# Delta-rule outputs for two chunks at once: state products first, masked-score products behind them, as two tiles side by side

## What is computed

```python
def step(S, inp):
    qd, kc, val, att, kt, cd = inp
    v_new = val - jnp.einsum('bhcd,bhde->bhce', kc, S)
    o = jnp.einsum('bhcd,bhde->bhce', qd, S) + jnp.einsum('bhij,bhje->bhie', att, v_new)
    S = S * cd[..., None, None] + jnp.einsum('bhcd,bhce->bhde', kt, v_new)
    return S, o
...
_, o = lax.scan(step, S0, xs)
```

## Time and profile before

| | |
|---|---|
| median of 3 runs | 1151.25 us (1151.17 to 1151.34) |
| the profiled execution | 1147.58 us, of which its span is 1145.8 us |
| busy in the span | PE 1117.3 us (98%), PEld 850.9 (74%), DVE 601.9 (53%), ACT 515.0 (45%), POOL 194.8 (17%) |
| the granted clock of TensorE over the span | 0.994 |
| the stretch of the delta rule's loop | about 146 to 172 us |

### The profile page before, as it was taken

One profiled execution on the slowest core, in us unless ns is written; L12 is line 12 of the kernel. 1 busy time (PEld: TensorE's weight loads), 2 busy tenths in 40 slices (PEclk: granted clock), 3 DMA queues, 4 the chain that ended last, 5 costly groups with the idle time before them and its releaser, 6 DMA issues.

```text
span 1145.8 us, 18715 instructions
## 1 busy us (share of the span) xinstructions
PE 1117.3 (98%) x7673; PEld 850.9 (74%) x7673; DVE 601.9 (53%) x885; ACT 515.0 (45%) x851; POOL 194.8 (17%) x132
## 2 busy tenths in 40 slices
PE   8999999999899999999999999999999999999996
PEld 7987778999688888878888885666666666666663
DVE  5988666879865695695656642222222222222223
ACT  6666553755364665745556342222222222222223
POOL 1339950422554140400000000000000000000000
PEclk9999999999899999999999999999999999999998
DMA  9862724567648656564448579999999999999994
GB/s 312 271 219 81 289 82 170 198 232 283 220 149 291 221 178 232 162 228 156 147 148 325 191 280 421 421 423 423 425 422 420 424 424 422 426 422 423 426 422 182
DMA packets 82700, 332.04 MB, mean 290 GB/s; under 512 B 4555, under 2 KB 6926, under 8 KB 66110
## 3 DMA queue, kind: packets, MB, share of 16 engines
q1 hardware_dynamic: 81236, 328.43, 74.1%
q0 software_dynamic: 1088, 2.34, 1.1%
q10 hardware_dynamic: 298, 0.11, 0.0%
HBM read 329.83 MB, written 1.05 MB: 289 GB/s over the span
## 4 chain that ended last, share of the span: by engine, by line
PE 77%; DVE 8%; DMA 7%; POOL 3%; issue 2%; ACT 2%; SPq 1%; DVEq 0%; ACTq 0%; POOLq 0%
PE bank L1113 18%; PE bank L446 11%; PE bank L448 10%; PE bank L447 10%; PE bank L1132 9%; PE bank L1103 5%; DMA ring<-in_w_exp_down 3%; POOL ring L2671 3%; DMA ring<-in_w_ada 2%; DVE ring_r L1847 2%; DMA ring<-in_w_in 2%; DVE arena L1927 2%; PE bank L1160 1%; PE bank L573 1%; PE bank L1161 1%
## 5 line engine op out<-in xcount | busy, mean ns | idle before, releaser
L1847 DVE TENSOR_TENSOR ring_r<-ring,arena_r 128x2048 fp32r<-128x2048 f32 x93 | 226.2, 2442 | 127.4 <-ACT arena_r L1333 125.7
L1333 ACT ACTIVATE arena_r<-ring 128x2048 fp32r<-128x2048 f32 x93 | 177.3, 1916 | 149.0 <-PE bank L448 69.7
L2671 POOL TENSOR_TENSOR ring<-ring 128x512 f32<-128x512 f32 x84 | 146.2, 1765 | 219.6 <-ACT ring L1424 191.6
L448 PE MATMUL bank<-arena_r,actT_r 128*128 128x512 f32 x384 | 150.5, 392 | 0.0
L446 PE MATMUL bank<-arena_r,tok_r 128*128 128x512 f32 x352 | 140.7, 400 | 1.7 <-DVE con L2312 1.7
L447 PE MATMUL bank<-ring_r,tok_r 128*128 128x512 f32 x352 | 138.2, 393 | 0.0
L2484 DVE TENSOR_TENSOR arena<-bank,arena 64x512 f32<-64x512 f32 x62 | 42.7, 688 | 175.3 <-PE bank L1132 174.6
L446 PE MATMUL bank<-tok_r,arena_r 128*128 128x256 f32 x352 | 99.5, 283 | 1.8 <-DVE actT_r L1864 1.2
L448 PE MATMUL bank<-tok_r,ring_r 128*128 128x256 f32 x352 | 98.3, 279 | 0.0
L447 PE MATMUL bank<-actT_r,arena_r 128*128 128x256 f32 x352 | 98.2, 279 | 0.0
L1304 ACT ACTIVATE arena<-bank 128x512 f32<-128x512 f32 (+5 forms) x123 | 54.4, 469 | 86.5 <-PE bank L1120 50.3
(11 more groups left out here) (426 smaller groups left out, 1833.1 us busy)
## 6 DMA issues: line engine op xcount, KB each, us to landing
ring<-in_w_in SPq DMA_DIRECT2D x22, 2048.0 KB, 9.2
ring<-in_w_exp_down SPq DMA_DIRECT2D x22, 2048.0 KB, 21.4
ring<-in_w_exp_gate SPq DMA_DIRECT2D x21, 2048.0 KB, 22.0
arena<-in_w_exp_up SPq DMA_DIRECT2D x21, 2048.0 KB, 23.6
ring<-in_w_ff SPq DMA_DIRECT2D x16, 2048.0 KB, 7.9
ring<-in_w_ada SPq DMA_DIRECT2D x12, 2048.0 KB, 10.9
arena<-in_w_exp_gate SPq DMA_DIRECT2D x11, 2048.0 KB, 21.6
arena<-in_w_exp_down SPq DMA_DIRECT2D x10, 2048.0 KB, 21.3
```

Source lines behind the costliest of these rows:

```text
L448: return mm(o, l[1], r[0], start=False, stop=stop)
L1333: A(hi, w, ACT.Copy).then_inc(S["w_high"], 1)
L1847: TT(half(i, ringR)[0], w, hi.bitcast(fp32), ALU.subtract).then_inc(S["w_rest"], 1)
L2671: i = nc.gpsimd.tensor_tensor(w[:, k, :], w[:, k, :], w[:, k + n, :], ALU.add)
```

## The change

`do0` to `do3` become two jobs, `do0` and `do1`, one for each half. A job is issued behind `sn1` (for the first half) and behind `vp3` and its fillers (for the second). It first runs all state products of the half, head by head, the two chunks alternating, and then all masked-score products, the two chunks alternating. The two chunks write to partitions 0 to 63 and 64 to 127 of one bank. Since chunk 2's state product now comes after the attention values and the first transposes of the finished tokens, the second state buffer moves to a place that those don't overwrite. ScalarE copies 128 partitions by 512 twice instead of 64 partitions by 512 four times. VectorE waits for one copy instead of two.

```diff
-        states = [KBE[:, 0:512], AT[:, 0:512]]
+        states = [KBE[:, 0:512], qT[:, 512:1024]]
...
+            def chunk_outputs(t):
+                bk = begin(f"do{t}")
+                chunks = [(2 * t + x, C * x) for x in range(2) if 2 * t + x]
+                for h in range(DH):
+                    for n, r in chunks:
+                        mm(bk[r:r + C, h * P:(h + 1) * P], block_cols(qdT)(4 * t + h, r),
+                           states[(n - 1) % 2][:, h * P:(h + 1) * P], start=(h == 0), stop=False, skip_group_check=True)
+                for h in range(DH):
+                    for r in (0, C):
+                        i = mm(bk[r:r + C, h * P:(h + 1) * P], within(MT)(4 * t + h, r), block_rows(VN)(4 * t + h, r),
+                               start=(h == 0 and t == 0 and r == 0), stop=(h == DH - 1), skip_group_check=True)
+                end(i, f"do{t}")
...
-                bk = begin(f"do{n}")
-                for h in range(DH):
-                    o = (4 * t + h) * P
-                    if n:
-                        mm(bk[r:r + C, h * P:(h + 1) * P], qdT[:, o + r:o + r + C], old[:, h * P:(h + 1) * P],
-                           start=True, stop=False)
-                    i = mm(bk[r:r + C, h * P:(h + 1) * P], MT[r:r + C, (4 * t + h) * C:(4 * t + h + 1) * C],
-                           VN[r:r + C, o:o + P],
-                           start=(n == 0), stop=True)
-                end(i, f"do{n}")
-                if n == 0:
-                    prob_turn(range(4))
+                if n % 2:
+                    chunk_outputs(t)
+                else:
+                    prob_turn(range(4)) if n == 0 else None
...
-            def o_copy(n):
-                t, r = n // 2, C * (n % 2)
-                bk = wait_full(act, f"do{n}")
-                done(copy(odn[r:r + C, t * 512:(t + 1) * 512], bk[r:r + C, :]), f"do{n}")
+            def o_copy(t):
+                bk = wait_full(act, f"do{t}")
+                done(copy(odn[:, t * 512:(t + 1) * 512], bk[:, :]), f"do{t}")
...
-            o_copy(0)
             prob_copies((0, 2))
             prob_copies((4, 6))
-            o_copy(1)
+            o_copy(0)
...
             w_high(F0 + 2)
-            o_copy(2)
             w_high(F0 + 3)
             o_high(0)
-            o_copy(3)
+            o_copy(1)
             o_scale(1)
...
                     if n == 2:
-                        wait_full(dve, "do1")
+                        wait_full(dve, "do0")
...
             def o_squares(t):
-                for n in (2 * t, 2 * t + 1):
-                    wait_read(dve, f"do{n}")
+                wait_read(dve, f"do{t}")
```

## The result

The changed kernel is slower: over 20 executions of each, the ratio to the kernel before is 1.0024, 95% interval 1.0014 to 1.0034 (medians 1152.06 against 1148.74 us). Run again beside ten more, it was 1.0019 (1.0005 to 1.0033). The forecast was 2.1 us faster; the two ratios stand for 2.8 and 2.2 us slower, and their intervals reach from 0.6 to 3.9 us.

A forecast was written before the change was run, and what follows sets the result against it. TensorE, busy in all 26.0 us around the loop, was taken as the bound: 5.6 us less work, less waits of 1.7 + 0.2 + 1.6 = 3.5, gives 2.1; 1151.25 - 2.1 = 1149.15 us, range 1147.4 to 1150.9.

The forecast's parts named there:

- Price of the products: Output jobs: state and masked-score groups overlap at 1.02 us each, 2.04 per job, taking 5.6 us of work off TensorE.
- The rival without overlap: Output jobs: masked-score products don't run side by side, 0.85 us more per half, total 1150.0 or 1150.2; chance 0.10.
- the price for every change of tile: Output jobs: alternating tiles costs like a size change, `do1` 5.76 us, 1.9 us slower, 1153.2; chance 0.06.
- Shift of the first half: Up to new state 2: 3.90 us removed ahead of `sn2`, 2.04 added, so `sn2` starts 1.86 us earlier, at 157.46.
- the wait of 1.7: Behind `sn2`, TensorE idles 1.7 us until VectorE has formed state 2; `vp3` starts at 160.26.
- VectorE as the next bound: Second half: VectorE's list ends at 170.03, TensorE idles 1.6 us, first product with `w_out` starts at 170.13.
- The clock: Rival: TensorE falls to 1.2 GHz after the last wait, gain only 0.1 us (1151.1); chance 0.09 shared with later stages.
- the later stages: Rival: transfers ending the program shift by 1 us or more, at worst 2 us slower; chance 0.09 shared with clock.
- All of the gain through to the end: Behind the first product with `w_out`: lists are the same, loads move with TensorE, so all 2.08 us reaches the end.

The follow-up runs named there:

- the wait filled: Changed kernel plus eight idle products, result unread, ahead of the fourth chunk's wait for the state (`vp3`); ratio to the kernel before 0.9994 (0.9980 to 1.0007).
- the kernel with half the idle products: Changed kernel plus four idle products instead of eight ahead of the fourth chunk's wait, leaving 0.56 us of wait; ratio to the kernel before 0.9987 (0.9969 to 1.0006).
- the two-group version: Changed kernel with the third chunk's output products moved behind `sn2`, the fourth's left behind the transposes, in one bank; ratio to the kernel before 0.9986 (0.9975 to 0.9998).
- 16 idle products of 128 by 128 by 128: Changed kernel plus sixteen idle products behind the 1.65 us wait and ahead of `vp3`; ratio to the kernel before 1.0040 (1.0021 to 1.0058).
- the outputs in the old, alternating form: Kernel before, four separate output jobs kept, third chunk's output moved behind the first token transposes so the wait opens; ratio to the kernel before 1.0081 (1.0059 to 1.0103).
- Denser work just ahead: Changed kernel plus eight idle products ahead of `sn2`, the 1.65 us wait left as it was; ratio to the kernel before 1.0028 (1.0013 to 1.0042).

## Why the prediction was wrong, step by step

- **Price of the products: right.** 1.02 us each for 16 side-by-side records, at full clock, and 2.04 for the first job, as taken from the earlier trace rows. Both side-by-side groups at full clock stand in the trace with the wait filled (165.93, 166.95, 167.97). The rival without overlap is refuted: masked-score products of two row tiles into one bank take 1.02 (153.46 to 154.48), not 1.87. So is the price for every change of tile, 5.76 for such a group. Where the Trainium skill ("TensorEngine Tiling (Array Packing)", "Restrictions and Gotchas") says that row tiles can't access the same bank at the same time, the measurement decides, for tiles on the diagonal.
- **Shift of the first half, 1.86 us, and the wait of 1.7: right.** `sn2` at 157.46 and `vp3` at 160.27 against 157.46 and 160.26; the wait is 1.65.
- **VectorE as the next bound: right as a mechanism, where the clock stays up.** With the wait filled the product starts at 169.88, forecast 170.13, after 1.25 us of waiting, forecast 1.6. In the changed kernel itself it is hidden behind a slower TensorE.
- **The clock: this step failed.** The prediction had it among the rivals, with 0.09 shared with the later stages, and set it aside because in 113 to 117 us TensorE waited 1.6 us and kept 2.4 GHz. That one row was no evidence for a wait at another place: the clock keeps its level over some waits of about this length and falls over this one. It also looked for the fall behind the last wait only, and took its price, 1.95, from 3.9 us of work at half clock behind another wait. It came at the first wait, with `vp3`, the attention values and the outputs behind it, and lasted 13.7 us in one trace and 10.2 in the other. Against the trace with the wait filled (169.88) the price is 4.9 and 3.1 us. Where 2.1 us of gain were forecast, the first product with `w_out` starts 2.6 and 0.8 us later than before. The timed price, from ratios of 0.9994 with the wait filled and 1.0019 and 1.0024 without, is 2.9 to 3.4 us, give or take about 2.
- **All of the gain through to the end: about half seen in the timed ratios.** Where the first product came 2.0 to 2.3 us earlier in the traces, the ratios show 0.7 to 1.6 us (the kernel with half the idle products, 2.7 us earlier, shows 1.5), with intervals of about 1.5 us to each side; 3.5 us earlier showed as 2.4. Whether part is lost in later stages or in the scatter stays open.
- **Size of the error.** The median from which the difference was taken, 1151.25, came from three executions that all lay at the top of the scatter (1146.1 to 1151.34 over 20). The range, 1147.4 to 1150.9, missed the measured 1152.06 anyway; against the later median the gain forecast would be 1146.6.

## What to carry to other kernels

Work taken off the busiest engine can be what it did while it waited for another, as the third chunk's outputs were here; if it goes, leave real work of equal length in each wait that opens, as the two-group version does, instead of gathering all of it behind the last dependency. A wait of 1.65 us cost a further 3.1 to 4.9 here, since TensorE fell to half clock for 10 to 14 us of the work behind it. Price a new wait on TensorE with its clock at both levels, over as much of the following work, and don't take one harmless wait elsewhere as proof.

## What was not expected of the hardware

How long a fall lasts depends on what follows the wait. In the traces the clock was at half for 3.4 us where 16 idle products of 128 by 128 by 128 followed, for 10.2 and 13.7 with `vp3`, the attention values and the side-by-side outputs behind it, and for 23.9 with the outputs in the old, alternating form, the first 2.4 us of the products with `w_out` among them. TensorE was busy in all of the 13.7 and in 23.7 of the 23.9 us, at half clock. Near 306 us in the kernel before, the 3.9 us of the earlier trace rows are only what was left of the fall when work began again; the clock had been low for 2.9 us of the wait.

```profile
303.44:310.20 6.76, 3.84 (x11) 3.23 (x12) 6.31 (x14) 0.00 (x0) 2.78 (x2) 0.50 0.92 333
```

What made the difference between the wait of 1.65 us at 158.6, which lowers the clock, and those of 1.65 near 497, 1.6 near 116 and 1.25 near 168.6, which don't in these traces, stays open. Denser work just ahead did not prevent the fall in the one trace of it, and sixteen full-size products just behind did not prevent it either, but cut it short.
